# The first norm of a diffusion step: transposes ahead of conditioning, one fold of squares a chunk, the block's barrier ahead of three conditioning tiles, the first row in halves

## The reference, cut to what matters

```
m = silu(cond) @ w_ada + b_ada ;  sh1, sc1, g1, sh2, sc2, g2 = split(m)
h = rms_norm(x, norm1_gain) * (1 + sc1) + sh1
proj = h @ w_in            # then the mixers, the output projection, the MLP
```

## Time and profile before

| | us |
|---|---|
| timed runs | 1638.29, 1640.0, 1641.33; median 1640.0 |
| profiled execution | 1638.48, its span 1636.7 |
| TensorE matmul busy | 1593.8 (97%) |
| VectorE busy | 970.8 (59%) |
| ScalarE busy | 695.0 (42%) |
| mean granted clock of TensorE | 0.992 |

### The profile page before, as it was taken

The page is one execution under the profiler, slowest core; times in us unless marked ns, Lnnn a source line. Parts: engine busy times, 40 slices in busy tenths (PEclk is TensorE's granted clock), DMA queues, the critical chain, the costliest instruction groups (busy, mean ns, idle before and its releaser), DMA issues.

```text
span 1636.7 us, 25959 instructions
## 1 busy us (share of the span) xinstructions
PE 1593.8 (97%) x10844; PEld 1340.1 (82%) x10844; DVE 970.8 (59%) x1269; ACT 695.0 (42%) x998; POOL 0.2 (0%) x4
## 2 busy tenths in 40 slices
PE   6999999999999998989999999999999999999997
PEld 5788887787888777777888888888888888888886
DVE  7515555854773586678966666656664544454437
ACT  4434429535843863366654444445430122012103
POOL 0000000000000000000000000000000000000000
PEclk8999999999999999999999999999999999999999
DMA  9541334424233355222332232231651123113103
GB/s 379 203 167 52 108 104 167 140 75 149 96 125 103 132 204 203 88 74 100 139 116 77 96 115 76 97 115 71 244 238 67 49 116 115 50 66 116 58 0 129
DMA packets 65004, 197.33 MB, mean 121 GB/s; under 512 B 8720, under 2 KB 18960, under 8 KB 64656
## 3 DMA queue, kind: packets, MB, share of 16 engines
q1 hardware_dynamic: 62176, 185.27, 30.9%
q10 hardware_dynamic: 2736, 10.73, 1.9%
HBM read 137.77 MB, written 55.58 MB: 118 GB/s over the span
## 4 chain that ended last, share of the span: by engine, by line
PE 52%; DVE 2%; DMA 1%; ACT 0%; issue 0%; SPq 0%; DVEq 0%
PE bank L96 17%; PE bank L97 17%; PE bank L98 17%; DMA hid_raw<-hidden 1%; PE bank L1320 0%; DVE hid_lo L1129 0%; PE bank L762 0%; DVE x L1391 0%; DMA hidden<-c 0%; DVE y_tok L1419 0%; DVE down_lo L1135 0%; DVE c L941 0%; DVE c L943 0%; PE bank L875 0%; SPq L1105 0%
## 5 line engine op out<-in xcount | busy, mean ns | idle before, releaser
L96 PE MATMUL bank<-hid_hi,down_lo 128*128 128x512 f32 (+1 forms) x768 | 273.6, 356 | 2.7 <-DVE hid_lo L1129 1.2
L1391 DVE SCALAR_TENSOR_TENSOR x<-bank,mod,x 128x512 f32<-128x512 f32 (+1 forms) x216 | 142.1, 661 | 222.4 <-PE bank L98 222.3
L97 PE MATMUL bank<-hid_lo,down_hi 128*128 128x512 f32 (+1 forms) x768 | 272.7, 355 | 0.0
L98 PE MATMUL bank<-hid_hi,down_hi 128*128 128x512 f32 (+1 forms) x768 | 271.9, 354 | 0.0
L96 PE MATMUL bank<-h_lat_hi,in_lo 128*128 128x512 f32 x512 | 205.6, 402 | 5.0 <-DVE h_lat_lo L402 5.0
L97 PE MATMUL bank<-h_lat_lo,in_hi 128*128 128x512 f32 x512 | 200.5, 392 | 0.0
L98 PE MATMUL bank<-h_lat_hi,in_hi 128*128 128x512 f32 x512 | 200.5, 392 | 0.0
L1118 ACT ACTIVATE hid_hi<-hid_raw 128x1280 fp32r<-128x1280 f32 x32 | 40.7, 1274 | 297.3 <-DMA hid_raw<-hidden 297.3
L96 PEld LDWEIGHTS bank<-hid_hi,down_lo 128*128 128x128 f32 x768 | 145.3, 189 | 25.1 <-DVE x L1391 2.3
L98 PEld LDWEIGHTS bank<-hid_hi,down_hi 128*128 128x128 f32 x768 | 145.1, 189 | 20.4
L97 PEld LDWEIGHTS bank<-hid_lo,down_hi 128*128 128x128 f32 x768 | 145.3, 189 | 19.9
(11 more groups left out here) (269 smaller groups left out, 3221.8 us busy)
## 6 DMA issues: line engine op xcount, KB each, us to landing
hid_raw<-hidden SPq DMA_DIRECT2D x32, 640.0 KB, 7.5
in_raw<-in_w_in SPq DMA_DIRECT2D x32, 512.0 KB, 5.9
mx_ada_raw<-in_w_ada_rest SPq DMA_DIRECT2D x32, 512.0 KB, 5.3
up_raw<-in_w_ff SPq DMA_DIRECT2D x32, 512.0 KB, 4.3
hidden<-c SPq DMA_DIRECT2D x64, 256.0 KB, 2.0
down_raw<-in_w_ff SPq DMA_DIRECT2D x32, 512.0 KB, 7.1
proj<-mx_stage ACTq DMA_DIRECT2D x16, 640.0 KB, 3.9
x<-x_scratch SPq DMA_DIRECT2D x16, 640.0 KB, 6.2
```

The source lines that it names most:

```text
L96: nc.tensor.matmul(out, w_lo, x_hi, start=start, stop=False)
L97: nc.tensor.matmul(out, w_hi, x_lo, start=False, stop=False)
L98: return nc.tensor.matmul(out, w_hi, x_hi, start=False, stop=stop)
L1391: nc.vector.scalar_tensor_tensor(xs, self.unit_bank(u)[:, 0:tn], g.m(40 + m, int(b > 0)), xs, ALU.mult, ALU.add).then_inc(self.unit_added[ ...
```

## The change

1. Conditioning leaves the chunk loop. All ten chunks are turned first; then TensorE clears bank 4 with one matmul of zeros, conditions two tiles, and three more behind the spreading of the first two groups. The last three tiles are conditioned at the head of the second block. Their DMAs now stand behind the two `w_in` tiles on SP's queue.
2. VectorE folds the squares once (eight rows to four), and TensorE sums four rows with four matmuls instead of two. ScalarE's square of chunk c waits for the sums of chunk c-2 instead of their fold.
3. In the second block ScalarE copies the whole bank (128x256, cleared before) in one instruction, TensorE turns the rows, and VectorE makes the amplitudes between the scaling of row 0 and that of row 1.
4. Row 0 gets its high and low parts in halves of 512 tokens, and TensorE takes the first half for both tiles of weights, then the second.

```diff
@@ sync
             for k in range(KT):
-                sp.dma_start(ada[:, k, :], a["w_ada"][1, k, :, :]).then_inc(ada_in[k], 16)
-            sp.wait_ge(turned, 7)
-            for s in range(2):
-                sp.dma_start(g.in_ring.raw[:, s, :], a["w_in"][s, :, :]).then_inc(g.in_ring.raw_in[s], 16)
+                if k == FirstNorm.EARLY_CONDITIONS:
+                    sp.wait_ge(turned, 7)
+                    for s in range(2):
+                        sp.dma_start(g.in_ring.raw[:, s, :], a["w_in"][s, :, :]).then_inc(g.in_ring.raw_in[s], 16)
+                sp.dma_start(g.ada_first[:, k, :], a["w_ada"][1, k, :, :]).then_inc(g.ada_in[k], 16)
@@ scalar
                 if c >= 2:
-                    act.wait_ge(added, c - 1)
+                    act.wait_ge(summed, c - 1)
...
-                if c == CHUNKS - 2:
-                    split_weights(nc, act, None, 0, 0, g.in_ring)
-            act.wait_ge(conditioned, 1)
-            act.wait_ge(zeroed, 1)
-            for j in range(4):
-                nc.scalar.activation(rows[32 * j:32 * j + 2, :], g.bank[4][32 * j:32 * j + 2, 0:REST], ACT.Copy
-                                     ).then_inc(rows_ready, 1)
+                if c >= CHUNKS - 2:
+                    split_weights(nc, act, None, 0, c - (CHUNKS - 2), g.in_ring)
             take_root(1)
-            split_weights(nc, act, None, 0, 1, g.in_ring)
@@ tensor, sums
-                for i in range(2):
-                    last = nc.tensor.matmul(g.bank[SUM_BANKS[part]][:, at_c:at_c + 1], sq_sum[:, c % 2, i, :], g.ones[:, 0:1],
-                                            start=(i == 0), stop=(i == 1))
+                for i in range(4):
+                    last = nc.tensor.matmul(g.bank[SUM_BANKS[part]][:, at_c:at_c + 1], sq[:, c % 2, i, :], g.ones[:, 0:1],
+                                            start=(i == 0), stop=(i == 3))
@@ tensor, order
                 turn(c)
-                if 2 <= c < EARLY_CHUNKS + 2:
+                if c >= 2:
                     sums(c - 2)
-                if c >= EARLY_CHUNKS:
-                    for i in range(2):
-                        condition(2 * (c - EARLY_CHUNKS) + i)
-            sums(EARLY_CHUNKS)
-            sums(EARLY_CHUNKS + 1)
+            pe.wait_ge(zeroed, 1)
+            FirstNorm.clear_rows(nc, g, FirstNorm.AMP_BANK)
+            FirstNorm.condition(nc, g, pe, range(2))
+            sums(CHUNKS - 2)
             pe.wait_ge(rstd_ready, 1)
             for b in range(2):
                 spread_block(b)
-            sums(CHUNKS - 2)
+            FirstNorm.condition(nc, g, pe, range(2, FirstNorm.EARLY_CONDITIONS))
             sums(CHUNKS - 1)
...
@@ vector, add_up
                 nc.vector.tensor_tensor(sq[:, s, 0:4, :], sq[:, s, 0:4, :], sq[:, s, 4:8, :], ALU.add
-                                        ).then_inc(halved, 1)
...
-                nc.vector.tensor_tensor(sq_sum[:, s, :, :], sq[:, s, 0:2, :], sq[:, s, 2:4, :], ALU.add
                                         ).then_inc(added, 1)
@@ FirstNorm
+    def clear_rows(nc, g, bank):
+
+        return nc.tensor.matmul(g.bank[bank][:, 0:REST], g.mod_rows[:, 0:P], g.mod_rows[:, :], start=True, stop=True)
...
+        act.wait_ge(self.amp_conditioned, 1)
+        nc.scalar.activation(g.mod_rows[:, :], g.bank[self.AMP_BANK][:, 0:REST], ACT.Copy).then_inc(self.amp_rows, 1)
+        act.wait_ge(self.amp_ready, 2)
+        for half in self.HALVES:
+            high(0, 1, half)
...
         scale(0, 1)
-        for k in range(1, KT):
+        dve.wait_ge(self.amp_turned, 1)
+        modulation_add(nc, g, g.bank[self.AMP_BANK], REST, 8, 2).then_inc(self.amp_ready, 1)
+        dve.wait_ge(self.amp_ready, 1)
+        nc.vector.scalar_tensor_tensor(g.amp1[:, :, :], g.mod[:, 8:16, :], 1.0,
...
+        scale(1, 1)
+        for i, half in enumerate(self.HALVES):
+            low(0, 1, half, i + 1)
+        for k in range(2, KT):
             scale(k, 1)
             low(k - 1, 1)
...
+        self.condition(nc, g, pe, range(self.EARLY_CONDITIONS, KT)).then_inc(self.amp_conditioned, 1)
+        pe.wait_ge(self.amp_rows, 1)
+        for b in range(2):
+            last = nc.tensor.transpose(g.bank[self.AMP_BANK][:, REST + b * P:REST + (b + 1) * P],
+                                       g.mod_rows[:, b * P:(b + 1) * P], g.ident[:, :])
+        last.then_inc(self.amp_turned, 1)
...
+        for b in (1, 2):
+            pe.wait_ge(self.lo_done[1], b)
+            for s in range(2):
+                step(s, b, 0)
```

More of the change, by code:

```diff
@@ L136, in modulation_and_input @@
         cond_s, x, rstd, root = g.cond_s, g.x_first, g.rstd, g.root
-        ada = at(nc, "ada", [P, KT, D_MODEL], F32, 0)
         x_tok = at(nc, "x_tok", [P, CHUNKS, D_MODEL], F32, 64)
         sq = at(nc, "x_sq", [P, 2, KT, P], F32, 104.125)
-        sq_sum = at(nc, "x_sq_sum", [P, 2, 2, P], F32, 112.125)
         pos = at(nc, "pos", [P, POS_COLS], F32, 114.125)
-        rows = at(nc, "mod_rows_first", [P, REST], F32, 116.125)
         cond = at(nc, "cond", [P, KT, 2], F32, 118.125)
         consts_in, pos_in, cond_in, cond_ready = sem("consts_in"), sem("pos_in"), sem("cond_in"), sem("cond_ready")
-        ada_in = [sem(f"ada_in{k}") for k in range(KT)]
         x_in = [sem(f"x_in{c}") for c in range(CHUNKS)]
-        turned, moved, squared, halved, added, summed = (
-            sem(n) for n in ("turned", "moved", "squared", "halved", "added", "summed"))
+        turned, moved, squared, added, summed = (sem(n) for n in ("turned", "moved", "squared", "added", "summed"))
         rooted, rstd_ready, spread, rstd_all_ready = (
             sem(n) for n in ("rooted", "rstd_ready", "spread", "rstd_all_ready"))
-        setup, zeroed, conditioned, rows_ready, rows_turned, mod_ready = (
-            sem(n) for n in ("setup", "rows_zeroed", "conditioned", "rows_ready", "rows_turned", "mod_ready"))
+        setup, zeroed = sem("setup"), sem("rows_zeroed")
         PAIRS_OF_BANKS = ((0, 1), (2, 3), (6, 7))
@@ L245, in _ @@
             pe.wait_ge(g.constants_ready, 1)
[L246 to L250, removed]
             def spread_block(b):
@@ L354, with condition @@
     CONDITION_AFTER, ROWS_AFTER, TURN_AFTER = 1, 5, 6
-    ROW_BANK = 7
+    AMP_BANK, ROW_BANK = 4, 7
+    EARLY_CONDITIONS = 5
+    HALVES = (slice(0, LAT // 2), slice(LAT // 2, LAT))
+    @staticmethod
+    def clear_rows(nc, g, bank):
+        return nc.tensor.matmul(g.bank[bank][:, 0:REST], g.mod_rows[:, 0:P], g.mod_rows[:, :], start=True, stop=True)
+    @staticmethod
+    def condition(nc, g, pe, tiles):
+        for k in tiles:
+            pe.wait_ge(g.ada_in[k], 16)
+            last = condition_rows(nc, g, g.bank[FirstNorm.AMP_BANK], g.ada_first[:, k, :], k, REST)
+        return last
     def __init__(self, nc, g, sem):
@@ L371, in scalar, with high @@
         nc, g = self.nc, self.g
-        def high(k, c):
-            n = SEGS[c][1]
+        def high(k, c, part=None):
+            part = part or slice(0, SEGS[c][1])
             act.wait_ge(self.normed[c], k + 1)
-            nc.scalar.activation(g.h_hi[c][:, k, 0:n], g.h_raw[c][:, k, 0:n], ACT.Copy, scale=g.amp1[:, k, c:c + 1]
+            nc.scalar.activation(g.h_hi[c][:, k, part], g.h_raw[c][:, k, part], ACT.Copy, scale=g.amp1[:, k, c:c + 1]
                                  ).then_inc(self.hi_done[c], 1)
+        act.wait_ge(self.amp_conditioned, 1)
[3 more added lines that the diff above has]
+            high(0, 1, half)
         for k in range(KT):
-            high(k, 1)
+            if k:
+                high(k, 1)
             if k == self.ROWS_AFTER:
@@ L434, in step @@
                 last.then_inc(signal(s, b), 1)
-        for k in range(KT):
-            pe.wait_ge(self.lo_done[1], k + 1)
-            for s in range(2):
-                if k == 0:
-                    pe.wait_ge(w.lo_ready[s], 1)
-                for b in (1, 2):
-                    step(s, b, k)
+        self.condition(nc, g, pe, range(self.EARLY_CONDITIONS, KT)).then_inc(self.amp_conditioned, 1)
[5 more added lines that the diff above has]
+        for s in range(2):
+            pe.wait_ge(w.lo_ready[s], 1)
+        for b in (1, 2):
+            pe.wait_ge(self.lo_done[1], b)
+            for s in range(2):
+                step(s, b, 0)
+        for k in range(KT):
+            if k:
+                pe.wait_ge(self.lo_done[1], k + 2)
+                for s in range(2):
+                    for b in (1, 2):
+                        step(s, b, k)
             if k == self.CONDITION_AFTER:
@@ L2508, in backbone_step @@
     g.root, g.rstd = at(nc, "root", [P, CHUNKS], F32, 190), at(nc, "rstd", [P, CHUNKS], F32, 190.125)
+    g.ada_first = at(nc, "ada", [P, KT, D_MODEL], F32, 0)
     g.proj = nc.dram_tensor("proj", [IN_BLOCKS, P, TOKENS], F32, kind="Internal").ap()
@@ L2524, in backbone_step @@
         g.in_ring, g.shift_in = Ring(nc, "in_", 80.125, sem), sem("shift_in")
+        g.ada_in = [sem(f"ada_in{k}") for k in range(KT)]
```

27 lines of the change are left out of this document (10 added, 17 removed).

## The result

The changed kernel takes **1648.72 us** in the median (1647.65 to 1654.21), the kernel before 1640.15; the ratio is 1.0056 [1.0044, 1.0068]. It is slower by 0.56%, some nine us. The forecast, 1638.8, and its range to 1645.2 did not hold this; rival (a), which the prediction put at 1646.1, is what happened, and it cost more than that. Two executions among the experiments, 2644.66 and 3255.03, stand far above all others and are in no ratio.

What follows compares the result with a forecast made beforehand. TensorE's long run of products was taken to bound the kernel, so its start decides. Loop and tail put block end 2.35 us earlier, amplitudes lose 1.1, first product 1.24 earlier: 1640.0 - 1.2 = 1638.8 us, range 1636.2 to 1645.2.

Steps and rivals of the forecast that it cites:

- rival (a): Chunk loop and tail: without conditioning the clock falls and stays down; 7.3 on the forecast, 1646.1 us; chance 0.30.
- 5.1 us are won here, if the clock stays at 2.4 GHz: Chunk loop: the last move starts at 25.6 instead of 30.71, provided TensorE keeps its full clock.
- TensorE is now busy nearly all the time: Chunk loop: argument against a falling clock, together with more transposes passing in each us.
- A list of waits beyond 60 us names none of TensorE's: After the first 60 us: product follows product, so nothing later was taken to change the time.
- the whole effect: Start of the products: how far the first product moves, plus TensorE's clock during the first products.
- The loop's term: Chunk loop: one fold less and twice the sums give 2.0 us a chunk, last move at 25.6; 5.1 us won.
- The tail's term: Tail of the block: TensorE's queue is late, last sums end at 32.6, block end 35.1, 2.35 us earlier.
- The amplitudes: After the barrier: block's end to first product takes 5.3 against 4.24; 1.1 us lost, first product at 40.45.
- SP's queue: DMA order: three `ada` tiles behind the `w_in` tiles let these land near 26 instead of 30.1.
- rival (c): SP's queue: the `w_in` tiles come no earlier; first product at 42.05, 1640.4 us; chance 0.09.
- The sum: Whole kernel: profiled 1638.48 - 1.24 = 1637.2; by the median 1640.0 - 1.2 = 1638.8 us, 0.07% less.
- 2.1 was kept: First products: low clock loses 2.1 us as before the change, within a possible loss from 0 to 3.4.

## Why the prediction was wrong, step by step

**The step that failed** is the condition in "5.1 us are won here, if the clock stays at 2.4 GHz", and the argument against rival (a): "TensorE is now busy nearly all the time". The earlier trace rows already held the counter-evidence, 20 to 22 with TensorE busy throughout on transposes and one-column sums and the clock at 0.50; the prediction quoted it and weighed it at 0.30. The changed kernel and the one with one-column matmuls show TensorE busy throughout and the clock at 0.50. The rule quoted from the Trainium skill, "TensorE: Matmul & The Clock Gate", "Part 4: PE-mode transpose", pointed the right way: this trace agrees with it through the loop, 2.00 busy of 2 at 0.50. The trace with two folds differs, at 1.00 from 26.2 to 29.7 with nothing else in the loop.

**Rival (a) was priced too low**, because it let the clock fall where it had fallen before, some 18 us in. It fell between 12 and 14, so that the six steps from the move of chunk 3 to that of chunk 9 were low, and a part of the one before, not three and a part: at 3.31 (predicted 3.4) instead of 2.0 a step, the last move came 8.4 after the 25.6 that was worked out. The tail at the lower level then took 11.6 from the last move to the end of the sums, where 7.0 were worked out for the full one: another 4.6, of which 4.1 are the clock (with it held, the same order took 7.5). The prediction had 2.95 for this and let the clock come back with the second sums; it came back behind the spreading. Together loop and tail are 13.0, and the first product came 12.9 later than the forecast's 40.45. Where the clock falls in a loop of this kind is not fixed: with the same loop it fell after 18 in the trace of before and by 14 in the kernel with halves.

**A list was read too far.** "A list of waits beyond 60 us names none of TensorE's" holds for 60 to 140 only. Further on the trace of before has

```profile
616.67 0.80 PE L96 MATMUL bank<-mx_early_lat_hi,mx_out_lo 128*128 128x512 f32 x1 [3.79 <-DMA mx_early_lat_lo<-mix_lo]
...
712.15 0.55 PE L96 MATMUL bank<-mx_early_ctx_hi,mx_out_lo 128*128 128x256 f32 x1 [3.33 <-DVE mx_out_lo L2373]
```

and more such waits, 3.3 and 4.8 us long at the second place in different kernels. So the start of the products and the clock there are not "the whole effect": the 11.7 us at the first product were 10.9 near 612, 10.4 near 694 and 9.4 at the end. Differences of one or two us in the time can't be put down to the first 60 us alone.

**The loop's term was right** once its condition is met: 25.6 was worked out for the last move, 25.37 measured with one wide matmul a chunk, 26.60 with two.

**The tail's term was right** in its cause and 0.5 short in size: with the clock held, the old order took 7.5 from the last move to the end of the last sums. The clearing matmul is 0.3 of that: it lasts 0.68 and holds the next back for 0.6, where 0.3 was taken. From the last sums to the block's end it was 2.4, by the forecast 2.5.

**The amplitudes** cost what was worked out: from the block's end to the first product 5.37 (47.98 to 53.35), by the forecast 5.3.

**SP's queue** did what was expected: near 26 was forecast, 26.1 measured with the clock held, so rival (c) falls. In the changed kernel itself it was 27.6, since the seventh chunk was turned late.

**The sum**: with the clock held by wide passes and nothing else altered the kernel takes 1638.51, near the forecast's 1638.8. That agreement is luck in part. Its first product starts at 41.87, 1.4 after the 40.45 of the forecast (the wide passes make each step 0.17 longer, and the tail is 0.5 longer), and the products then run for 6.0 us at the lower level, 3.0 lost where 2.1 was kept. By the forecast's own sum that is 1641.1; the profiled execution took 1640.05, the slowest of ten.

## What to carry to other kernels

Before taking wide matmuls out of a stretch whose other TensorE work is transposes and one-column sums, price the stretch at both clock levels, from its first step on; that TensorE is busy is no argument for the higher one. An otherwise useless 128-column matmul or two a step can be cheap: 0.2 us a chunk here, against 1.3 lost. Where work is moved off a loop, look at what then queues behind it: the same conditioning put ahead of the last sums made the first product 1.9 us later than behind them. And look for waits over the whole run before a gain at its start is counted as a gain at its end.

## What the runs showed of the hardware

- TensorE busy for 2.00 of 2 us was granted 0.50 over some 22 us with transposes and one-column matmuls alone (12.8 to 35.3), and 1.00 with one or two 128-column matmuls more a chunk. Two one-column matmuls in their place left it at 0.50. In all six traces with such wide matmuls the loop stayed at 1.00; in all six without them the clock fell in it.
- The clock also came back among transposes and one-column sums alone (two folds, 26.2 to 29.7), and 5 us passed between the end of the first conditioning and its return in the changed kernel (38.3 to 43.5), 1.4 in the kernel before (24.2 to 25.6).
- The same instructions in the loop lost the clock at different places: the trace of before still showed 1.00 at 16 to 18, the one with halves 0.50 at 14 to 16.
- Filling an empty wait with wide matmuls kept the clock up behind it (products 0.39 instead of 0.63), but the 2.3 us so won ahead of the shift's conditioning did not arrive at the end of the kernel before. In its trace TensorE waited 2.87 for VectorE 1150 us later, and the clock fell in that wait for 6.8 us.
